# Sequence 0's score products ahead of a block's barrier, W_out's first rows split on VectorE, and the down-projection's last two weight blocks in tile order

## What is computed

```
h = rms_norm(x); x_r, q, k, v, g_a, g_b = h @ w_in
y_a = rg_lru(conv4(x_r));  o = softmax(q1 k1) v - lam * softmax(q2 k2) v      # 8 heads, two maps each
x = x + (sigmoid(g_a) * y_a + sigmoid(g_b) * rms_norm(o)) @ w_out
up = conv3(rms_norm(x) @ w_up)
x = x + (gelu(up[:, :3072]) * up[:, 3072:]) @ w_down
y = rms_norm(x)
```

## Time and profile before

| what | value |
| --- | --- |
| median of 3 runs | 1893.4 us |
| the profiled execution's own time | 1896.46 us |
| its span in the profile | 1894.6 us |
| mean granted clock of TensorE | 0.991 |
| TensorE / weight load busy | 97% / 88% |
| VectorE / ScalarE / GpSimd busy | 63% / 54% / 18% |
| DMA, mean | 129 GB/s |

### The profile page before, as it was taken

The page is one execution under the profiler, slowest core; times in us unless marked ns, Lnnn a source line. Parts: engine busy times, 40 slices in busy tenths (PEclk is TensorE's granted clock), DMA queues, the critical chain, the costliest instruction groups (busy, mean ns, idle before and its releaser), DMA issues. The chain is left out here.

```text
span 1894.6 us, 39813 instructions
## 1 busy us (share of the span) xinstructions
PE 1836.9 (97%) x13704; PEld 1661.4 (88%) x13704; DVE 1190.1 (63%) x2268; ACT 1022.1 (54%) x1956; POOL 338.1 (18%) x299
## 2 busy tenths in 40 slices
PE   6999999999999999979999889999999999999998
PEld 6999999999999999966666689999999999888886
DVE  6776767676767676775553787555655566454454
ACT  5775757474747575762334655455444554334353
POOL 0000000000000000021100065565556552000000
PEclk9999999999999999989999899999999999999999
DMA  6421112121112121389999412222232224757572
GB/s 198 161 66 51 57 49 59 47 61 56 53 54 60 54 64 50 100 287 327 375 377 335 138 47 80 81 80 69 70 90 70 78 69 174 240 182 243 169 251 71
DMA packets 217998, 243.47 MB, mean 129 GB/s; under 512 B 40549, under 2 KB 178757, under 8 KB 217909
## 3 DMA queue, kind: packets, MB, share of 16 engines
q1 hardware_dynamic: 214601, 233.88, 37.7%
q0 software_dynamic: 2096, 7.60, 1.1%
q10 hardware_dynamic: 1212, 0.81, 0.1%
HBM read 205.48 MB, written 42.02 MB: 131 GB/s over the span
## 5 line engine op out<-in xcount | busy, mean ns | idle before, releaser
L1298 PE MATMUL ps<-h_hi,w_hi 128*128 128x384 f32 (+1 forms) x1152 | 387.0, 336 | 5.0 <-DVEq L1013 3.4
L1298 PE MATMUL ps<-h_hi,w_lo 128*128 128x384 f32 (+1 forms) x1152 | 376.8, 327 | 0.0
L1298 PE MATMUL ps<-h_lo,w_hi 128*128 128x384 f32 (+1 forms) x1152 | 376.7, 327 | 0.0
L2714 PE MATMUL ps<-d_hi,d_a 128*128 128x512 f32 x816 | 255.8, 389 | 2.1 <-DVE d_a L3040 2.1
L1298 PEld LDWEIGHTS ps<-h_hi,w_hi 128*128 128x128 f32 x1152 | 217.3, 189 | 9.0 <-issue 4.0
L1298 PEld LDWEIGHTS ps<-h_lo,w_hi 128*128 128x128 f32 x1152 | 217.4, 189 | 0.6
L1298 PEld LDWEIGHTS ps<-h_hi,w_lo 128*128 128x128 f32 x1152 | 217.0, 188 | 0.0
L2714 PEld LDWEIGHTS ps<-d_hi,d_a 128*128 128x128 f32 x816 | 153.1, 188 | 35.1 <-DVE d_lo L3031 2.5
L3031 DVE TENSOR_TENSOR d_lo<-d_raw,d_hi 128x1024 fp32r<-128x1024 f32 x72 | 88.2, 1225 | 132.0 <-ACT d_hi L2852 131.9
L2714 PE MATMUL ps<-d_lo,d_a 128*128 128x512 f32 x432 | 168.1, 389 | 0.0
L2852 ACT ACTIVATE d_hi<-d_raw 128x1024 fp32r<-128x1024 f32 x72 | 76.4, 1061 | 155.3 <-PE ps L2714 145.4
(11 more groups left out here) (446 smaller groups left out, 4938.2 us busy)
## 6 DMA issues: line engine op xcount, KB each, us to landing
d_raw<-in_w_down SPq DMA_DIRECT2D x72, 512.0 KB, 3.6
k<-in_cache_k SPq DMA_DIRECT2D x64, 512.0 KB, 6.5
vr<-in_cache_v SPq DMA_DIRECT2D x56, 512.0 KB, 6.5
w_raw<-in_w_in SPq DMA_DIRECT2D x48, 512.0 KB, 3.9
act_dram<-f_yv SPq DMA_DIRECT2D x24, 512.0 KB, 3.9
f_rG<-in_w_up SPq DMA_DIRECT2D x23, 512.0 KB, 3.9
f_rV<-in_w_up SPq DMA_DIRECT2D x23, 512.0 KB, 4.0
d_araw<-act_dram SPq DMA_DIRECT2D x48, 192.0 KB, 3.8
```

Source lines behind the costliest of these rows:

```text
L1298: last_ = pe.matmul(bank(s)[:, 0:n], w[:, W_SLOT[g], k, :], x[:, k, off:off + n], start=(k == 0 and i == 0), stop=(k == KT - 1 and i == 2))
L2714: l_ = pe.matmul(ps[:, DGROUP_BANKS[g][2 * q + hf], :], a, w[:, cols], start=(start and i == 0), stop=(stop and i == len(pairs) - 1))
```

## The change

Three things change.

1. TensorE makes sequence 0's 128 score matmuls with past keys (`score_block`) at the end of its list of the heads' block. It waits for the last users of PSUM slots 0 and 1, for the last reading of the heads' scores, for 16 more increments of `s_fill` (each copy of `spread_queries` now raises it) and for `kt_done`. The 8 matmuls with the new keys stay behind the barrier.
2. W_out's row blocks 0 and 1 are split by VectorE and no longer by GpSimd. VectorE's order for sequence 0 becomes: low part of `m`, row blocks 0, 1, 2, a key page, softmax, a key page, `signs`, C, and on as before.
3. In the last round of the down-projection block 3 is done in block order too; only blocks 4 and 5 (`DLAST` = 2) go tile by tile. The very last tile is added, squared, scaled and stored in halves: the first half's square is taken before the last addition, its sum enters as the bias of the root. VectorE's order at the end becomes: additions 0 to 3, scaling of tile 6, addition 4, scaling of the sampled tile, the small `half_set` step, addition 5, and two half scalings.

```diff
@@ -617,7 +617,7 @@
...
             pool.wait_ge(qlo_done, 3 * H)
-            spread_queries(pool.tensor_copy, c, 0, (2, 3))
+            spread_queries(lambda dst, src: pool.tensor_copy(dst, src).then_inc(c.s_fill, 1), c, 0, (2, 3))
@@ -994,7 +994,7 @@
...
                         act.wait_ge(qlo_done, 3 * H)
-                        spread_queries(lambda dst, src: act.activation(dst, src, ACT.Copy), c, 0, (0, 1))
+                        spread_queries(lambda dst, src: act.activation(dst, src, ACT.Copy).then_inc(c.s_fill, 1), c, 0, (0, 1))
                 assert chain[0] == ACT_LINKS, ("ACT_LINKS", chain[0])
@@ -1421,6 +1421,25 @@
...
+            for slot in (0, 1):
+                released(pe, H - 1, max((x for x in RING if RING[x] % NSLOT == slot), key=lambda x: RING[x]))
+            pe.wait_ge(ttr_done, cur(H - 1, 16, 15))
+            pe.wait_ge(c.s_fill, 4 + 4 * NQ)
+            pe.wait_ge(c.kt_done, NPAGES)
+            for e in range(2):
+                for j in range(NQ):
+                    score_block(pe, ps, c.qd, c.k0, e, j)
+def score_block(pe, ps, qd, keys, e, j):
+    for h in range(HH):
+        J = NQ * (HH * e + h) + j
+        for i in range(NQ):
+            part = slice(32 * i, 32 * i + 32)
+            pe.matmul(ps[32 * h:32 * h + 32, i, 0:32 * NPAGES], qd[part, J, :], keys[part, :, 32 * J:32 * J + 32],
+                      start=(e == 0 and j == 0), stop=(e == 1 and j == NQ - 1))
@@ -1438,7 +1457,7 @@
...
 HALF = 3 * KT
-POOL_W = (0, 1, 3, 6)
+POOL_W = (3, 6)
 DVE_W = tuple(k for k in KS if k not in POOL_W)
@@ -1618,8 +1637,6 @@
...
-            weight_low(0)
-            weight_low(1)
             weight_low(3)
@@ -1731,16 +1748,11 @@
...
                     pe.wait_ge(ttr_done, (NQ + 1) * b)
-                for e in range(2):
-                    for j in range(NQ):
-                        for h in range(HH):
-                            J = NQ * (HH * e + h) + j
-                            for i in range(NQ):
-                                part = slice(32 * i, 32 * i + 32)
-                                pe.matmul(S[32 * h:32 * h + 32, i, :], qd[part, J, :],
-                                          keys[part, :, 32 * J:32 * J + 32],
-                                          start=(e == 0 and j == 0), stop=(e == 1 and j == NQ - 1))
-                        fill(b, among.get(NQ * e + j, 0))
+                if b > 0:
+                    for e in range(2):
+                        for j in range(NQ):
+                            score_block(pe, ps, qd, keys, e, j)
+                            fill(b, among.get(NQ * e + j, 0))
                 if b > 0:
@@ -2176,16 +2188,17 @@
...
-            signs()
             dve.wait_ge(mhi_done, 1)
...
                .then_inc(mplo_done, 1)
-            weight_low(2)
+            for k in (0, 1, 2):
+                weight_low(k)
             turn_keys(1, (0,))
...
             turn_keys(1, (1,))
+            signs()
             weights(0)
@@ -2289,6 +2302,7 @@
...
 DT, DR = 3, 6
+DLAST = 2
 ND = NP // DR
@@ -2342,7 +2356,7 @@
...
     stc = sb("f_stc", [128, 2, NST], F32, 222304)
-    fst = sb("y_st", [128, NT, 3], F32, 222464)
+    fst = sb("y_st", [128, NT + 1, 3], F32, 222464)
     fold = sb("y_fold", [128, NS], F32, 222592)
@@ -2562,14 +2577,19 @@
...
                 sp.wait_ge(yn_done, i + 1)
-                if D_NORMS[i] < NT - 1:
-                    t = D_NORMS[i]
+                t = D_NORMS[i]
+                if i == NT - 1:
+                    for hf in range(2):
+                        cols = slice(512 * hf, 512 * (hf + 1))
+                        sp.wait_ge(yn_done, i + 1 + hf)
+                        sp.dma_start(yp[128 * t:128 * (t + 1), cols], yn[i % 3][:, cols]).then_inc(y_last, 16)
+                elif D_NORMS[i] < NT - 1:
                     sp.dma_start(yp[128 * t:128 * (t + 1), :], yn[i % 3][:, :]).then_inc(y_last, 16)
...
                 sp.wait_ge(y_out[u], 32)
-            sp.wait_ge(y_last, 48)
+            sp.wait_ge(y_last, 64)
             sp.wait_ge(st_out, 64 * NP)
@@ -2719,7 +2739,7 @@
...
                     for hf in range(2):
-                        for r in range(DR - DT, DR):
+                        for r in range(DR - DLAST, DR):
                             if q == 0 and hf == 0:
@@ -2734,7 +2754,7 @@
...
             def down(g, it):
-                for r in range(DR - DT if g == 2 and ends(it) else DR):
+                for r in range(DR - DLAST if g == 2 and ends(it) else DR):
                     pe.wait_ge(dlo_done, block_count(g, it, r))
@@ -2917,12 +2937,31 @@
...
                     act.wait_ge(fold_done, 1)
-                else:
+                elif i < NT - 1:
                     act.wait_ge(add_done, 2 * D_TILES.index(t) + 2)
+                if i == NT - 1:
+                    last_square(t)
+                    return
                 act.activation(junk[0:n, :], final_rows(i)[0:n], ACT.Square, accum_out=fst[0:n, t, 0:1])\
...
                 act.activation(fst[0:n, t, 1:2], fst[0:n, t, 0:1], ACT.Sqrt, bias=eps[0:n, :], scale=1.0 / D)\
+                   .then_inc(std_done, 1)
+            def half_square(t, hf):
+                cols = slice(512 * hf, 512 * (hf + 1))
+                act.wait_ge(add_done, 2 * NT - 1 + hf)
+                return act.activation(junk[:, cols], final_rows(NT - 1)[:, cols], ACT.Square,
+                                      accum_out=fst[:, NT if hf == 0 else t, 0:1])
+            def last_square(t):
+                half_square(t, 0).then_inc(std_done, 1)
+                half_square(t, 1).then_inc(std_done, 1)
+                act.wait_ge(std_done, 2 * NT)
+                act.wait_ge(half_set, 1)
+                act.activation(fst[:, t, 1:2], fst[:, t, 0:1], ACT.Sqrt, bias=fst[:, NT, 1:2], scale=1.0 / D)\
                    .then_inc(std_done, 1)
@@ -3121,13 +3160,20 @@
...
                 n = NS if t == NT - 1 else 128
-                dve.wait_ge(std_done, 2 * i + 2)
+                dve.wait_ge(std_done, 2 * i + 2 + (i == NT - 1))
                 dve.reciprocal(fst[0:n, t, 2:3], fst[0:n, t, 1:2]).then_inc(chain, 1)
...
                     dve.wait_ge(y_out[i % 3], 16 * (i // 3))
+                if i == NT - 1:
+                    for hf in range(2):
+                        cols = slice(512 * hf, 512 * (hf + 1))
+                        dve.scalar_tensor_tensor(out=yn[i % 3][:, cols], in0=final_rows(i)[:, cols],
+                                                 scalar=fst[:, t, 2:3], in1=gain[:, cols], op0=ALU.mult,
+                                                 op1=ALU.mult).then_inc(yn_done, 1)
+                    return
                 dve.scalar_tensor_tensor(out=yn[i % 3][0:n, :], in0=final_rows(i)[0:n], scalar=fst[0:n, t, 2:3],
@@ -3149,9 +3195,11 @@
...
             norm(NT - 3)
-            for e in range(4, 6):
-                add(2, e)
+            add(2, 4)
             norm(NT - 2)
+            dve.wait_ge(std_done, 2 * NT - 1)
+            dve.tensor_scalar(fst[:, NT, 1:2], fst[:, NT, 0:1], 1.0 / D, EPS, ALU.mult, ALU.add).then_inc(half_set, 1)
+            add(2, 5)
             norm(NT - 1)
```

More of the change, by code:

```diff
@@ L2404, in mixer @@
     fold_done = sem("y_fold_done")
+    half_set = sem("y_half_set")
     chain = sem("u_chain")
@@ L3193 @@
     "td_done add_done x2_in0 x2_in1 x2_in2 y_g_in y_std_done y_yn_done "
-    "y_out0 y_out1 y_out2 y_last y_fold_set y_fold_done").split()
+    "y_out0 y_out1 y_out2 y_last y_fold_set y_fold_done y_half_set").split()
 class Shared:
```

## The result

The changed kernel takes 1895.89 us in the median of 20 executions (1892.17 to 1899.58), the kernel before 1892.18 us in 20 beside them (1888.37 to 1899.45). The ratio is 1.0019, with a 95% interval of 1.0010 to 1.0027: **3.6 us slower**. Measured once more beside other kernels it was 1.0012 (1.0001 to 1.0024), 2.3 us. The forecast was 1892.8 us, 0.6 us less than before and no change that can be told; a difference of 0.19% could be told, as the interval shows. The time lies inside the range (1887.8 to 1896.8), but on the other side of the kernel before. Two executions of the kernel before that stood far off (2019.1 and 3842.5 us) are left out of every ratio.

A forecast was written before the change was run, and what follows sets the result against it. TensorE, busy 1836.9 of 1894.6 us, was taken as the bound, so only its idle or slowly clocked stretches could be won. Seam +1.5 and end -2.1 gave -0.6: 1892.8 us against 1893.4, range 1887.8 to 1896.8.

The forecast's parts named there:

- step 3: Seam, weights' products to scores(1): 10.9 us before, slow clock expected again with phase moved, 1.2 us taken off.
- 4.4 us of clock: Seam, weights' products to scores(1): the most that full clock instead of 0.50 could save; bounds 0 and 4.4.
- Step 1: Seam, barrier L597: score products start at 832.5, barrier opens at 841.2 against 835.5, 5.7 us later for every other engine.
- no idle over 0.5 us ahead of the score products: Seam, TensorE: a sign that the forecast is right; idle there was to fall from 3.6 to 0.4 us.
- Step 2: Seam, VectorE's chain behind the barrier: C ready 13.3 us after opening, at 854.5, so weights' products start 2.7 us later.
- 2.2 us of port lock: Seam, VectorE's W_out subtractions: one takes 3.39 instead of 1.22 us beside GpSimd's, adding 2.2 us before C is ready.
- The sum of the seam: Seam: +2.7 us for later weights' products less 1.2 us of clock, +1.5 us; bounds about -5 and +4.2.
- The end: Last blocks: 2.12 us TensorE stall covered, VectorE's end -1.7, last DMA -0.4: -2.1 us, bounds -1.3 and -2.7.
- Rival D: At the end: another wait takes the stall's place and the end gives nothing; 1894.9 us, chance 0.08.
- C: Rival, seam: barrier waits for TensorE's code, opens at 844.4, weights' products later; +4.2 us, 1897.6 us, chance 0.15.
- my case: The forecast itself: seam +1.5 us, end -2.1 us, 1892.8 us; chance 0.52.
- B: Rival, seam: busy TensorE has full clock and no code gap, barrier at 838.3; -4.5 us, 1888.9 us, chance 0.25.

The follow-up runs named there:

- before_again: The kernel before, unaltered, run again for a second profile: ratio 0.9995 to the kernel before.
- tail_only: The kernel before with part 3 alone (DLAST = 2 and the last tile in halves): ratio 0.9986, -2.6 us.
- dlast_only: The kernel before with DLAST = 2 and the two loops that use it, last tile whole: ratio 0.9985, -2.8 us.
- whole_again: The whole change once more, unaltered, for a second profile: ratio 1.0012 to the kernel before, +2.3 us.
- seam_only: The kernel before with parts 1 and 2 (128 scores ahead, new low parts), the end as before: ratio 1.0034, +6.4 us.
- signs_first: The whole change with `signs` back ahead of the low part of `m`: ratio 1.0017 to the kernel before, +3.2 us.
- scores_only: The kernel before with part 1 alone (128 score matmuls ahead of the barrier), old low parts and end: ratio 1.0023, +4.4 us.
- all_scores: The kernel before with the new end and all 128 score matmuls ahead of the barrier, old low parts: ratio 0.9989, -2.1 us.
- all_again: all_scores run once more: ratio 0.9998 to the kernel before, -0.4 us.
- few_scores: The kernel before with the new end and 32 of 128 score matmuls ahead of the barrier, old low parts: ratio 0.9964, -6.8 us.
- half_scores: The kernel before with the new end and 64 of 128 score matmuls ahead of the barrier, old low parts: ratio 0.9967, -6.2 us.
- none_scores: The kernel before with the new end and the added waits and increments, no score matmuls ahead of the barrier: ratio 0.9982, -3.4 us.
- split_only: The kernel before with part 2 alone (new division of low parts), scores behind the barrier, old end: ratio 0.9999, -0.2 us.

## Why the forecast was wrong

From the start of TensorE's last product of L1396 (its next product starts 2.14 us later in every profile) to C's products and to scores(1), in us:

| seam | profiles | C's products | scores(1) | between |
| --- | --- | --- | --- | --- |
| old | before, before_again, tail_only, dlast_only | 28.0, 27.3, 26.5, 27.6 | 45.8, 41.0, 40.9, 41.3 | 17.9, 13.8, 14.4, 13.8 |
| changed | whole change, whole_again, seam_only, signs_first | 28.5, 28.2, 29.3, 29.6 | 45.5, 43.7, 46.4, 46.2 | 17.0, 15.4, 17.1, 16.6 |
| 128 ahead, old low parts | scores_only, all_scores, all_again | 30.1, 30.3, 29.6 | 47.9, 44.5, 43.8 | 17.9, 14.3, 14.2 |
| 32, 64 ahead, old low parts | few_scores, half_scores | 24.9, 25.0 | 39.2, 42.9 | 14.3, 17.9 |

**The step that failed is step 3**, "I expect the slow clock again, but with its phase moved; I take 1.2 off". In the pair of profiles it is right (17.9 to 17.0). But the 17.9 of the profiled execution is not the usual level of the kernel before: the three other profiles with the old seam have 13.8 to 14.4, at full clock. Two more kernels have the scores behind the barrier, none_scores with 15.5 and split_only with 17.9. The two profiles at 17.9 are of executions 4.3 and 1.9 us above their kernel's median, the four at 13.8 to 15.5 of executions 0.7 to 2.2 us below theirs. I had the 4.4 us of clock as a bound below, as something the change might win; it was something that the faster executions of before already had, and that the change puts at risk. Against before_again, tail_only and dlast_only this term is +1.0 to +3.3, not -1.2; between executions below their median on both sides (17.0, 15.4 and 16.6 against 13.8, 14.4, 13.8 and 15.5) it is +2.0 in the mean. The same error stands in the sum: I took the 3.1 us by which the profiled execution stood over the median as a plain offset, when the earlier trace rows showed where a good part of them lay, in the very stretch that I was pricing.

**Step 1** was right. The score products start 8.7 us behind L1396's last product in all four profiles of the changed seam, set by the turned key pages (forecast 832.5, 8.6). TensorE's first product behind the barrier comes 4.6 to 5.9 us later than in the earlier trace rows on that scale, where 5.7 was forecast. The sign "no idle over 0.5 us ahead of the score products" failed without harm: 1.95 or 1.96 us stand there in three of the four profiles, as the heads' last products ended earlier. The gap ahead of the barrier was 1.43 us in the first profile, 2.52 in whole_again and 0.74 in signs_first, and seam_only's timeline has none (256 records in one run of 7.25 us); the Trainium skill's "mostly hidden" (Runtime: NRT & Kernel Launch, section Instruction fetch mechanics) fits the last alone, if these gaps are waits for code.

**Step 2** said 2.7 later for C's products; measured 0.2 to 3.1 (28.2 to 29.6 against 26.5 to 28.0), 1.6 in the mean. Whether its 2.2 us of port lock fall on VectorE changed between executions. In the profile of the change and in whole_again it fell on GpSimd, whose low part took 3.48 and 3.47 us, and C's products start 10.7 us behind the first product after the barrier. In seam_only and signs_first it fell on VectorE, whose three low parts took 5.67 and 5.66, and C's products start at 12.9 and 12.7; GpSimd had started 0.09 and 0.10 us ahead of VectorE's third low part there, and 0.02 ahead in the other two. The Trainium skill's rule that the two exclude each other (SBUF — State Buffer, section SBUF: two separate sides) agrees with both. seam_only's timeline:

```profile
841.53 5.67 DVE L2137 TENSOR_TENSOR wo_lo<-wo_raw,wo_hi 128x1024 fp32r<-128x1024 f32 x3
```

**The sum of the seam**: forecast +1.5, the profiles' means say +3.2 (45.5 against 42.3), the runs +6.4 (seam_only) and 4.9 to 6.2 (the whole change less the new end). By the mean clock (0.9906 against tail_only's 0.9932) 2.8 us of the latter are TensorE's clock, if the slope holds for them. From scores(1) to scores(7) the profiles show no difference (150.2 to 152.2 us in the six with the scores behind the barrier, 150.5 to 151.2 in the four of the change), so what was lost there was lost before scores(1). Four profiles on each side are too few to place the rest; that is open.

**The end** was forecast at -2.1 and measured -2.6 (interval -4.5 to -0.8). The stall goes, the addition is held by the sampled rows' scaling as worked out. Only the forecast's "0.65 us earlier" was a slip: it sets the end of the new addition (1887.05) against the start of the old (1887.70). Start to start its own numbers give 1.35, and the addition starts 0.84 us later behind TensorE's last product than before, as its numbers had it (1886.35 against 1885.5). From TensorE's last product to the end of the span it is 7.3 us before and after: the shorter steps and the DMA (2.3 to 1.8) pay for the held addition. Rival D falls, and no use of the halves can be told.

**Rivals.** C had the right sign and named the right place, but its opening at 844.0 was not reached: the four profiles give 840.1 to 841.4 on the scale of the earlier trace rows. Below 844.0 it put the loss under 0.2%, and the whole above 1893.4 from 840.2 on "with its clock", which I read as without the 1.2 us that my case took off. That is about what came: an opening within my bounds, no gain of clock, and 0.19%. B was wrong for 128 matmuls. For 32 and 64 its gain came and more, but not by its mechanism alone: half_scores has a gap of 0.91 us, and half clock to 857.5, and gains by C's products at 25.0. The number of matmuls, which I took as given, is where gain turns into loss. That the time fell inside the range was luck of its width: the direction was wrong.

## What to carry to other kernels

Fill an engine's wait for a barrier only with as much work as ends before the others arrive; here 32 or 64 of 128 matmuls gained 2.8 to 4.2 us over none (none_scores and tail_only), and all of them lost 0.5 to 3.0, as what comes ahead of the barrier held every engine. Before a forecast stands on a profiled execution, look at where it differs from the median: if its slow stretch is the one that is changed, price the change against both levels. Of the versions here, 32 matmuls ahead with the old low parts and the new end has the lowest ratio (few_scores, 1887.3 us, 0.9964 of before), with half_scores (0.9967) inside its interval; DLAST = 2 alone gives as much as the whole new end, as far as can be told.

## What the hardware showed that I had not expected

The place of TensorE's instructions can be worth more than the whole change. 26 matmuls of 8 columns in an idle stretch made the kernel 10.6 us slower, and in both kernels with 26 added matmuls the same waits without a semaphore came up in the score products of sequence after sequence (2.9, 1.3 and 0.7 to 0.9 us in the first three of each), although everything there is as before. That they are waits for code is what the 16 KB packets in the earlier trace rows and the shift suggest; no run tells it from another cause that hangs on the place of the instructions.

Idle time of TensorE ahead of C (three pieces of 3.1 to 3.2, 0.2 to 1.9 and 1.4 to 2.2 us in the four profiles of the change, against one of 2.19 in before_again) goes with half clock on what follows C in most profiles, but not all. scores_only and all_scores have the same 6.5 us hole, and the stretch behind C takes 17.9 us in the one and 14.3 in the other. Both have granted clock 0.50 from about 844 on; in all_scores it ends at 854.1, as C's products begin, in scores_only only at 861.4. A single profile says which level an execution had, not which it usually has.
